# First projection: opening put in another order, and the low halves of later weight quarters moved from GpSimd to VectorE

## The reference

```python
h = _f32(_rmsnorm(x, ab_norm_g[i]))
proj = h @ _f32(ab_w_in[i])
z_a, xbc, dt_raw, z_b, q, k, v, ig, fg, og = jnp.split(proj, AB_SPLITS, axis=-1)
```

## Time and profile before

| what | us |
|---|---|
| median of 3 runs | 1732.99 |
| lowest and highest of them | 1732.58, 1734.13 |
| the profiled execution, device time | 1737.41 |
| its span in the trace | 1735.7 |
| busy in the span: PE, DVE, ACT, POOL | 1594.0, 901.5, 633.9, 529.8 |
| mean granted TensorE clock over the span | 0.957 |

### The profile page before, as it was taken

One profiled execution on the slowest core, in us unless ns is written; L12 is line 12 of the kernel. 1 busy time (PEld: TensorE's weight loads), 2 busy tenths in 40 slices (PEclk: granted clock), 3 DMA queues, 4 the chain that ended last, 5 costly groups with the idle time before them and its releaser, 6 DMA issues. The chain is left out here.

```text
span 1735.7 us, 23902 instructions
## 1 busy us (share of the span) xinstructions
PE 1594.0 (92%) x9329; PEld 1363.0 (79%) x9329; DVE 901.5 (52%) x1449; ACT 633.9 (37%) x1221; POOL 529.8 (31%) x324
## 2 busy tenths in 40 slices
PE   5899999999999669999699975999999999999797
PEld 5679989898999558778588854787888887888686
DVE  5646748585733357787434327134554333553533
ACT  5243434343531024433322214224454432555421
POOL 5534454444443135555100014022122103222111
PEclk9899999999999789999799987999999999999999
DMA  4034243232432414433214042012111102111632
GB/s 149 1 105 141 67 129 110 86 126 69 158 110 86 139 59 158 137 101 127 97 49 145 1 157 89 13 35 57 62 49 55 43 7 79 37 44 49 231 132 97
DMA packets 131592, 155.59 MB, mean 90 GB/s; under 512 B 7762, under 2 KB 108246, under 8 KB 130462
## 3 DMA queue, kind: packets, MB, share of 16 engines
q1 hardware_dynamic: 131486, 154.13, 26.9%
HBM read 109.97 MB, written 44.14 MB: 89 GB/s over the span
## 5 line engine op out<-in xcount | busy, mean ns | idle before, releaser
L311 POOL TENSOR_TENSOR p_w_lo<-p_b,p_w_hi 128x1024 fp32r<-128x1024 f32 x67 | 168.4, 2514 | 198.1 <-ACT p_w_hi L379 198.1
L1800 POOL TENSOR_TENSOR a_w_lo<-a_w_raw,a_w_hi 128x1024 fp32r<-128x1024 f32 x40 | 96.3, 2409 | 294.9 <-DVE a_w_hi L2020 256.9
L2030 DVE CUSTOM_DVE_ANT_0 a_s<-a_ps,a_neg_dist 128x256 f32<-128x256 f32 (+7 forms) x128 | 91.9, 756 | 151.5 <-PE a_ps L2221 151.5
L2203 PE MATMUL a_ps<-a_h_hi,a_w_hi 128*128 128x512 f32 x384 | 163.3, 425 | 5.5 <-DVE a_h_lo L1999 5.5
L2203 PE MATMUL a_ps<-a_h_lo,a_w_hi 128*128 128x512 f32 x384 | 152.7, 398 | 0.0
L2203 PE MATMUL a_ps<-a_h_hi,a_w_lo 128*128 128x512 f32 x384 | 152.6, 397 | 0.0
L1913 ACT ACTIVATE a_s<-a_s,a_nm 128x256 f32<-128x256 f32 (+7 forms) x128 | 98.5, 771 | 139.3 <-DVE a_nm L2030 139.3
L706 PE MATMUL p_bank<-p_w_hi,p_hi_s 128*128 128x256 f32 x512 | 144.9, 283 | 0.0
L706 PE MATMUL p_bank<-p_w_lo,p_hi_s 128*128 128x256 f32 x512 | 144.9, 283 | 0.0
L706 PE MATMUL p_bank<-p_w_hi,p_lo_s 128*128 128x256 f32 x512 | 144.9, 283 | 0.0
L602 DVE SCALAR_TENSOR_TENSOR p_c_acc<-p_out_raw,p_cols,p_c_acc 128x1024 f32<-128x1024 f32 x60 | 123.9, 2072 | 9.0 <-ACT p_c_acc L410 7.5
(11 more groups left out here) (351 smaller groups left out, 3958.6 us busy)
## 6 DMA issues: line engine op xcount, KB each, us to landing
p_b<-in_ab_w_in SPq DMA_DIRECT2D x52, 512.0 KB, 4.0
tok<-p_out_raw SPq DMA_DIRECT2D x64, 256.0 KB, 2.5
a_w_raw<-in_c_w_in SPq DMA_DIRECT2D x32, 512.0 KB, 4.2
k_gz<-tok SPq DMA_DIRECT2D x8, 1536.0 KB, 9.9
feat<-p_c_acc SPq DMA_DIRECT2D x20, 512.0 KB, 3.0
k_fe<-feat SPq DMA_DIRECT2D x8, 1280.0 KB, 6.7
y_w_raw<-in_ab_w_out SPq DMA_DIRECT2D x8, 1024.0 KB, 5.2
a_s<-x SPq DMA_DIRECT2D x12, 512.0 KB, 4.8
```

The costliest lines, as they stand in the source:

```text
L311: gp.tensor_tensor(w_lo[s % SLOTS][:, :, :], operand(n, split_of(n, p))[:, :, :], w_hi[s % SLOTS][:, :, :].bitcast(F32), ALU.subtract).the ...
L1800: gp.tensor_tensor(w_lo[:, w, :], w_raw[u % W_RAW][:, :], w_hi[:, w, :].bitcast(F32), ALU.subtract).then_inc(S["l_wlo"], 1)
L2030: dve.tensor_tensor_reduce(s[:, 0:W], score[j][:, 0:W], neg_dist[:, SEQ - W:SEQ], -SLOPES[h], 3e38, ALU.add, ALU.min, nm[n % 2][:, j:j + 1 ...
L2203: mm = pe.matmul(o, x, y, start=(k == 0 and q == 0), stop=(k == KT - 1 and q == 2))
```

## The change

It touches `projection_ab` alone.

- **Loads.** Tile 1 of x is loaded ahead of the small rows of gains and taps, tiles 2 and 3 ahead of the first weight quarter, tile 5 ahead of the third, tiles 6 and 7 ahead of the gate columns.
- **Scales.** Sum and scale get a column per tile, so that a square no longer waits for the scale two tiles before. `scale_of` is parted into the scale and `diagonal`, and the scales of tiles 6 and 7 stand ahead of the diagonal of tile 6 and of `low_weights(2)`.
- **Low halves of tiles.** GpSimd's `low_tile` is gone; VectorE's `low_late` makes all five of a tile, right behind its sums.
- **Low halves of weights.** GpSimd makes those of s = 0 to 9. Those of s = 10 to 91 are made by VectorE, one at each of seven places of its order in a block.
- **Gates.** `gates(0)` stands behind product 3 and not 5; it waits for the last `gained` instead of for a free bank and uses a bank of the transposes. `keep_gates(0)` stands ahead of `keep_block0(0)`. `gates(1)` waits for six copies of block 0's results, as before.
- **Sums.** D21 is made ahead of `gained(4)`.
- **ScalarE.** Squares 2 and 3 stand ahead of the high halves of tiles 0 and 1, squares 6 and 7 ahead of those of tile 4, and `high_weights(4)` ahead of those of tile 7.
- **Waits.** Products 4 to 7 wait for a count of VectorE's low halves (25 of 28) instead of GpSimd's.

```diff
-        g_bank = [bank[1], bank[5]]
+        g_bank = [bank[6], bank[5]]
...
@@ -236,25 +236,25 @@
...
             load_x(0)
+            load_x(1)
             at = 0
             for r in rows:
                 sp.dma_start(row_in[at:at + r.shape[0], :], r).then_inc(S["rows_in"], 16)
                 at += r.shape[0]
-            load_x(1)
-            load_b(0, 0, 0)
             load_x(2)
             load_x(3)
+            load_b(0, 0, 0)
             load_b(0, 1, 0)
             load_x(4)
+            load_x(5)
             load_b(0, 0, 1)
             load_b(0, 1, 1)
-            load_x(5)
+            load_x(6)
+            load_x(7)
             with nc.allow_non_contiguous_dma(reason="24 gate columns"):
                 for c, w, o in ((C_DT, SSD_HEADS, 0), (C_IG, 2 * ML_HEADS, SSD_HEADS)):
                     sp.dma_start(g_raw[:, 0:KT, o:o + w], w_in[:, c:c + w].rearrange("(k p) n -> p k n", p=P)
                                  ).then_inc(S["g_landed"], 16)
-            load_x(6)
-            load_x(7)
...
@@ -293,17 +293,18 @@
...
             def scale_of(t):
-                r = rstd[t % 2][:, :]
+                r = rstd[:, t:t + 1]
                 gp.wait_ge(S["squared"], t + 1)
-                if t >= 2:
-                    gp.wait_ge(S["diag_ok"], t - 1)
-                gp.tensor_scalar(r, sumsq[t % 2][:, :], 1.0 / D, EPS, ALU.mult, ALU.add).then_inc(S["mean_ok"], 1)
+                gp.tensor_scalar(r, sumsq[:, t:t + 1], 1.0 / D, EPS, ALU.mult, ALU.add).then_inc(S["mean_ok"], 1)
                 gp.wait_ge(S["mean_ok"], t + 1)
                 gp.tensor_tensor(r, r, half[:, :], ALU.pow).then_inc(S["rstd_ok"], 1)
+
+            def diagonal(t):
                 gp.wait_ge(S["rstd_ok"], t + 1)
                 if t >= 2:
                     gp.wait_ge(S["x_T"], 2 * (t - 1))
-                gp.tensor_tensor(diag[t % 2][:, :], ident[:, :], r.broadcast_to([P, P]), ALU.mult).then_inc(S["diag_ok"], 1)
+                gp.tensor_tensor(diag[t % 2][:, :], ident[:, :], rstd[:, t:t + 1].broadcast_to([P, P]), ALU.mult
+                                 ).then_inc(S["diag_ok"], 1)
...
@@ -311,32 +312,21 @@
...
-            def low_tile(t):
-                u = t - 4
-                ts = slice(u * P, (u + 1) * P)
-                for i, (a, src) in enumerate((("22", h_f[t % 2][:, HK:KT, :]), ("s1", s1_f[t % 2][:, :, :]),
-                                              ("s4", raw_12[:, :, ts]))):
-                    gp.wait_ge(S["a_hi"], 8 + 5 * u + (1, 2, 5)[i])
-                    gp.tensor_tensor(A[a][1][:, :, ts], src, A[a][0][:, :, ts].bitcast(F32), ALU.subtract
-                                     ).then_inc(S["l_low"], 1)
-
-            scale_of(0)
-            scale_of(1)
+            for t in range(4):
+                scale_of(t)
+                diagonal(t)
             low_weights(0)
-            scale_of(2)
-            scale_of(3)
             low_weights(1)
             scale_of(4)
+            diagonal(4)
             scale_of(5)
+            diagonal(5)
+            scale_of(6)
+            scale_of(7)
+            diagonal(6)
             low_weights(2)
-            low_tile(4)
-            scale_of(6)
-            low_weights(3)
-            low_tile(5)
-            scale_of(7)
-            low_tile(6)
-            low_tile(7)
-            for s in range(4, STEPS):
+            diagonal(7)
+            for s in range(3, F0 + 2):
                 low_weights(s)
 
...
@@ -427,38 +414,37 @@
...
             square(0)
             square(1)
+            square(2)
+            high_early(0)
+            square(3)
+            high_early(1)
             high_weights(0)
-            high_early(0)
-            square(2)
-            high_early(1)
-            square(3)
             high_early(2)
             high_weights(1)
             high_early(3)
             square(4)
             square(5)
             high_weights(2)
+            square(6)
+            square(7)
             high_late(4)
-            square(6)
+            high_late(5)
             high_weights(3)
-            high_late(5)
-            square(7)
             high_late(6)
+            high_weights(4)
             high_late(7)
-            for s in range(4, F0):
-                high_weights(s)
-                if s == 5:
-                    keep_block0(0)
-                    keep_block0(1)
-                    keep_gates(0)
-                if s == 7:
-                    keep_block0(2)
+            high_weights(5)
+            keep_gates(0)
+            high_weights(6)
+            keep_block0(0)
+            keep_block0(1)
+            high_weights(7)
+            keep_block0(2)
             for s in range(F0, F0 + SLOTS):
                 high_weights(s)
...
@@ -529,8 +514,10 @@
             def low_late(t):
                 u = t - 4
                 ts = slice(u * P, (u + 1) * P)
-                for i, (a, src) in enumerate((("s3", h_f[t % 2][:, 0:HK, :]), ("s2", raw_11[:, :, ts]))):
-                    dve.wait_ge(S["a_hi"], 8 + 5 * u + 3 + i)
+                for i, (a, src) in enumerate((("22", h_f[t % 2][:, HK:KT, :]), ("s1", s1_f[t % 2][:, :, :]),
+                                              ("s3", h_f[t % 2][:, 0:HK, :]), ("s2", raw_11[:, :, ts]),
+                                              ("s4", raw_12[:, :, ts]))):
+                    dve.wait_ge(S["a_hi"], 8 + 5 * u + 1 + i)
                     dve.tensor_tensor(A[a][1][:, :, ts], src, A[a][0][:, :, ts].bitcast(F32), ALU.subtract
                                       ).then_inc(S["d_low"], 1)
...
@@ -602,6 +589,16 @@
...
+            def low_weights(s):
+                if s >= STEPS:
+                    return
+                n, p = step_at(s)
+                dve.wait_ge(S["a_whi"], s + 1)
+                if s == F0 + 2:
+                    dve.wait_ge(S["l_wlo"], F0 + 2)
+                dve.tensor_tensor(w_lo[s % SLOTS][:, :, :], operand(n, split_of(n, p))[:, :, :],
+                                  w_hi[s % SLOTS][:, :, :].bitcast(F32), ALU.subtract).then_inc(S["l_wlo"], 1)
...
@@ -610,46 +607,52 @@
...
             low_early(3)
+            sum_weights(0, "D21")
             gained(4)
             sums_of_tile(4)
+            low_late(4)
             gained(5)
-            low_late(4)
             sums_of_tile(5)
-            gained(6)
             low_late(5)
-            sums_of_tile(6)
             dve.wait_ge(S["g_landed"], 32)
             dve.tensor_tensor(g_raw[:, KT:, :], g_raw[:, HK:KT, :], g_raw[:, 0:HK, :], ALU.subtract).then_inc(S["g_diff"], 1)
             dve.wait_ge(S["g_diff"], 1)
             dve.tensor_copy(g_hi[:, :, :], g_raw[:, :, :]).then_inc(S["g_split"], 1)
             dve.wait_ge(S["g_split"], 1)
             dve.tensor_tensor(g_lo[:, :, :], g_raw[:, :, :], g_hi[:, :, :].bitcast(F32), ALU.subtract).then_inc(S["g_split_lo"], 1)
+            gained(6)
+            sums_of_tile(6)
+            low_late(6)
             gained(7)
-            low_late(6)
             sums_of_tile(7)
             low_late(7)
-            sum_weights(0, "D21")
             sum_weights(0, "T3")
             sum_weights(1, "T1")
             sum_weights(1, "T2")
             sum_weights(1, "T3")
             for n in range(1, nb):
                 turned = (lambda f: conv(n - 1, f)) if after(n, "f") else (lambda f: None)
+                low_weights(seq(n, "1") + 2)
                 turned(0)
                 turned(1)
+                low_weights(seq(n, "2") + 2)
                 quarters(n, C11)
                 turned(2)
+                low_weights(seq(n, "6") + 2)
                 quarters(n, U2)
                 sum_weights(n, "T4")
                 turned(3)
+                low_weights(seq(n, "7") + 2)
                 quarters(n, U3)
+                low_weights(seq(n, "5") + 2)
+                quarters(n, C22)
+                quarters(n, U4)
+                low_weights(seq(n, "4") + 2)
+                quarters(n, C21)
+                low_weights(seq(n, "3") + 2)
                 if n + 1 < nb:
                     sum_weights(n + 1, "T1")
                     sum_weights(n + 1, "T2")
-                quarters(n, C22)
-                quarters(n, U4)
-                quarters(n, C21)
-                if n + 1 < nb:
                     sum_weights(n + 1, "T3")
                 quarters(n, C12)
...
@@ -675,12 +678,13 @@
...
                 if n == 0:
-                    pe.wait_ge(*((S["d_low"], 7), (S["d_low"], 8), (S["d_low"], 8), (S["d_low"], 8), (S["l_low"], 11),
-                                 (S["l_low"], 11), (S["l_low"], 11), (S["l_low"], 11))[p])
-                if n == 1 and p in "1673":
-                    pe.wait_ge(*{"1": (S["g_staged"], 1), "6": (S["g_staged"], 2), "7": (S["d_low"], 16), "3": (S["l_low"], 12)}[p])
+                    pe.wait_ge(S["d_low"], 7 if p == 0 else 8 if p < 4 else 25)
+                    if p == 6:
+                        pe.wait_ge(S["g_staged"], 1)
```

(27 more changed lines are left out.)

## The result

| | kernel before | changed kernel |
|---|---|---|
| median, us | 1732.92 (1732.58 to 1734.13, 4 runs) | 1721.34 (1718.15 to 1722.98, 4 runs) |
| ratio to before, 95% interval | | 0.993 (0.9912 to 0.9947) |
| profiled execution, span, us | 1735.7 | 1719.5 |
| granted TensorE clock over the span | 0.957 | 0.961 |

The medians differ by 11.6 us (forecast: 14.1, to 1718.9), and the interval of the ratio spans 9.2 to 15.2 us. A second comparison on one chip, with 6 runs of the changed kernel and 23 of the one before, gave 1722.47 against 1734.81, 12.3 us, ratio 0.9926 (0.9907 to 0.9946).

What follows compares the result with a forecast made beforehand. TensorE bounds the long stretch, so time can be won in the opening. Block 1 moves from 111.4 to 97.3, 14.1 us earlier, with the long stretch costed at nothing: median 1733.0 to 1718.9, range 1710.5 to 1726.

Steps and rivals of the forecast that it cites:

- Product 0: Opening: VectorE's low halves alternate with GpSimd's weight halves at the port; product 0 starts at 25.4, 0.7 us later than before.
- a smooth slowing: Shared port: alternative to full blocking, slowing by 1.67 us an operation; product 0 would start at 23.2.
- The gates: Opening: TensorE waits 6.0 us at the gates for VectorE's chain, 28.8 us long, ending with the last `gained` at 62.4.
- Half pace: Behind the wait at the gates: TensorE loses 2.1 us at half pace; gates end at 70.0.
- Products 4 to 7, block 1: Five times 5.46 us from 70.0 with no wait ahead of products 4 to 7; block 1 starts at 97.3.
- The long stretch: From block 1 on: VectorE takes over 82 subtractions, busy at most 331 of 475 us; costed at nothing.
- The margin: Token block behind a feature block: low half for product 6 done at 23.8, needed at 28.8, 5.0 us in hand.
- The sum: Block 1 starts 14.1 us earlier and nothing behind it changes pace: median 1733.0 to 1718.9.
- The rival of no wait at the gates: GpSimd's operations fall where VectorE reads PSUM, 6 us held time and 2.1 half pace go: gain 22.2, 1710.8; chance 0.12.

Runs made afterwards that it cites:

- VectorE alone: All 92 weight halves made by VectorE, on top of the kernel with the other bank and halves 2 to 9 on VectorE: 1714.78 us, ratio 0.9879.
- the old loads: SyncE's loads in the order of before: in the changed kernel 1719.7 us; in the kernel with the copy repaired 1711.87 us.
- the move alone: Kernel before, with weight halves 10 to 91 made by VectorE in the order of the change: 1734.5 us, ratio 1.0004.
- the opening alone: Changed kernel without its move of weight halves: GpSimd makes all 92, VectorE's block order as before; 1720.11 us, ratio 0.9913.
- the other bank: Changed kernel with the first gates in a bank freed by tile 6's gains, product 4 waiting for their copy: 1719.16 us, ratio 0.9902.
- halves 2 to 9: Kernel with the other bank, and weight halves 2 to 9 made by VectorE as well: 1716.01 us, ratio 0.9885.
- the copy repaired: Kernel with all weight halves on VectorE, the copy of the gates moved behind tile 7's high halves: 1714.41 us, ratio 0.9874.

## Why the prediction was right

- **Product 0 (forecast 25.4, measured 25.39).** Giving TensorE its second and third tile earlier bought nothing, since VectorE's pair of low halves then met both of GpSimd's weight halves. The runs with VectorE alone (1.28 us for the pair, product 0 at 22.7) and the two with the old loads (0.9 us with GpSimd's halves, none without them) show that mechanism; a smooth slowing would have given 23.2 (the prediction writes of a slowing by 1.67 us; its 23.2 takes each of two operations to last 1.67, against 0.6 free). Six traces with this order of loads put product 0 at 25.2 to 25.4, so the hit is not luck.
- **The gates (62.4, 62.01; wait 6.0, 5.17).** From the end of `gained(4)` to that of `gained(7)` the chain took 28.2 us and not 28.8: the gate split took 1.0 (0.25, 0.31 and 0.46), where I had charged 1.3, and the three weight halves held it for 5.7 and not 6.2 (1.33 at 33.76, 2.2 at 46.88, 2.2 at 57.21). The other part of the smaller wait is TensorE itself, at product 3's end at 56.8 and not 56.4.
- **Half pace (2.1, 2.6).** From 62.01 to 70.07 the gates took 8.06 us for 5.46 of work. That 0.5 more cancels the 0.4 by which the gates came early, so product 4 at 70.07 is closer to the forecast than its two terms are.
- **Products 4 to 7, block 1 (97.3, 97.6).** Product 4 at 70.07 (70.0). No wait behind it; the copy of the gates, which had cost 4.04 us and half pace, is out of the way. The run with the gates behind product 5 brought it back.
- **The long stretch (no cost).** Shown from both sides: the move alone is worth 1.0004 (0.9992 to 1.0015), and the opening alone 0.9913. VectorE was busy 327 us (at most 331). The margin was mis-sized: in the third block the low half for the sixth product is ready 25.2 us after the block's start (at 201.2; block start 176.0), so 3.6 us in hand and not 5.0, because a convolution operation takes 1.28 and its run of three 3.9 instead of 3.5.
- **The sum (14.1).** In the traces the start of block 1 moved by 13.8 us and the first instruction of the stage behind the projection by 13.9 (590.79 to 576.92). The medians moved by 11.6 and 12.3. Two steps can hold the missing 2 us, and the runs do not tell them apart. One is the starting point: 111.4 is block 1 of a single execution, which was 4.4 us above its median, and the opening with the same code in the run of the move alone reached block 1 at 109.25, with 1.6 us less at half pace. From 109.25 the gain is 11.6 us to the first trace of the change and 11.9 to the second. The other is that nothing behind the projection changes: that part scatters from trace to trace by more than 2 us, see below. The intervals hold 14.1 us as well.

The rival of no wait at the gates was the right question asked too loosely. The wait did not go in either trace of the changed kernel; TensorE's wait there shrinks to 0.76 us when VectorE makes the halves itself and the copy of the gates stands farther back. What it is worth is read best at the start of product 4, which the clock behind that wait cannot move: 70.1 in the changed kernel (where the gates lose 2.6 at half pace ahead of it), 65.4 with the other bank, 64.6 with halves 2 to 9, 62.5 with all of them, 60.1 with the copy repaired. In the last two, product 0 itself starts 2.7 and 3.3 us earlier.

## What to carry to other kernels

Before you share work between VectorE and GpSimd, count their two-input SBUF operations as one queue: if VectorE's chain sets a wait, a 2.4 us operation of GpSimd in its middle costs more than doing it on VectorE in 1.22. Where a product must wait for a chain, put independent matmuls (here the gates) just ahead of it, and put the copy that frees them behind whatever the chain itself needs from ScalarE. Relief of an engine that nobody waits for, here 48 us of convolution time, was worth nothing by itself.
